# First stage: spreading the last linear steps over all half-steps of the banded attention

## The reference

```python
h = modulate(rmsnorm(x, norm1_g), shift1, scale1)
q, k, v, rw, gl = jnp.split(h @ w_in, IN_SPLITS, axis=-1)
q = apply_rope(q.reshape(B, L, N_Q_HEADS, HEAD_DIM), cos, sin)
k = apply_rope(k.reshape(B, L, N_KV_HEADS, HEAD_DIM), cos, sin)
ya = latent_window_attention(q, k, v, kc, vc, sink)
```

## Time and profile before

| what | value |
|---|---|
| median of 3 runs | 3562.92 us (3561.78 to 3563.11) |
| profiled execution, its time | 3547.06 us |
| profiled execution, its span | 3545.3 us |
| PE busy in the span | 3257.0 us (92%) |
| DVE, ACT, POOL busy | 1899.5, 1156.1, 1559.4 us |
| mean granted clock of PE | 0.948 |

### The profile page before, as it was taken

How to read it: one execution, slowest core, us unless ns; L and a number is a source line. 1 busy time by engine, 2 the same in 40 slices (tenths; PEclk the granted TensorE clock), 3 DMA queues, 4 the chain that set the end, 5 groups by cost and what they waited for, 6 DMA issues and landing times. The chain is left out here.

```text
span 3545.3 us, 46174 instructions
## 1 busy us (share of the span) xinstructions
PE 3257.0 (92%) x17972; PEld 2580.0 (73%) x17972; DVE 1899.5 (54%) x2664; ACT 1156.1 (33%) x2265; POOL 1559.4 (44%) x1195
## 2 busy tenths in 40 slices
PE   5888999999799999889999999999898999999796
PEld 2666787788598988667788878887675666777565
DVE  3278874545445455587733373337412666564736
ACT  4144441333333333431211021102223665134723
POOL 1114665456144341266666666666551001654432
PEclk8988899999899999999999999999997999999898
DMA  4335555232344342343333333334434321322112
GB/s 168 79 116 149 161 152 180 88 94 70 95 127 108 98 126 62 115 147 89 89 96 95 99 90 97 95 98 105 140 104 118 85 61 40 89 82 60 48 54 78
DMA packets 524317, 358.58 MB, mean 101 GB/s; under 512 B 92497, under 2 KB 477382, under 8 KB 524102
## 3 DMA queue, kind: packets, MB, share of 16 engines
q1 hardware_dynamic: 513446, 325.22, 31.9%
q0 software_dynamic: 4608, 16.78, 1.6%
q10 hardware_dynamic: 6048, 13.63, 1.1%
HBM read 276.85 MB, written 78.18 MB: 100 GB/s over the span
## 5 line engine op out<-in xcount | busy, mean ns | idle before, releaser
L2420 PE MATMUL psum<-place,place 128*128 128x512 f32 x2126 | 862.7, 406 | 82.5 <-POOL place L2398 35.7
L2421 PE MATMUL psum<-place,place 128*128 128x512 f32 x2126 | 842.8, 396 | 0.0
L2422 PE MATMUL psum<-place,place 128*128 128x512 f32 x2126 | 842.0, 396 | 0.0
L2396 POOL CAST place<-place 128x1024 fp32r<-128x1024 f32 (+3 forms) x302 | 303.5, 1005 | 1113.8 <-PE psum L2422 656.7
L2398 POOL TENSOR_TENSOR place<-place,place 128x1024 fp32r<-128x1024 f32 (+3 forms) x302 | 693.2, 2295 | 24.2
L2420 PEld LDWEIGHTS psum<-place,place 128*128 128x128 f32 x2126 | 408.6, 192 | 199.1 <-POOL place L2398 53.8
L2421 PEld LDWEIGHTS psum<-place,place 128*128 128x128 f32 x2126 | 408.8, 192 | 90.8 <-issue 7.5
L2422 PEld LDWEIGHTS psum<-place,place 128*128 128x128 f32 x2126 | 408.0, 192 | 87.9
L662 PE MATMUL psum<-place,place 128*128 128x512 f32 (+1 forms) x712 | 288.0, 405 | 22.3 <-issue 11.6
L663 PE MATMUL psum<-place,place 128*128 128x512 f32 (+1 forms) x712 | 272.8, 383 | 0.0
L664 PE MATMUL psum<-place,place 128*128 128x512 f32 (+1 forms) x712 | 272.4, 383 | 0.0
(11 more groups left out here) (326 smaller groups left out, 5471.8 us busy)
## 6 DMA issues: line engine op xcount, KB each, us to landing
place<-in_w_mlp_up SPq DMA_DIRECT2D x64, 512.0 KB, 4.0
place<-in_w_mlp_down SPq DMA_DIRECT2D x64, 512.0 KB, 4.0
place<-in_w_out SPq DMA_DIRECT2D x48, 512.0 KB, 4.0
chunked<-place SPq DMA_DIRECT2D x64, 320.0 KB, 3.6
place<-in_w_in SPq DMA_DIRECT2D x34, 512.0 KB, 5.7
solve<-in_w_ada POOLq DMA_DIRECT2D x32, 512.0 KB, 6.2
place<-in_lru_w_in SPq DMA_DIRECT2D x32, 512.0 KB, 4.0
place<-in_mla_w_in SPq DMA_DIRECT2D x30, 512.0 KB, 4.2
```

The costliest lines, as they stand in the source:

```text
L2396: nc.gpsimd.tensor_copy(hi, raw).then_inc(self.w_split, 1)
L2420: pe.matmul(ps, self.w_hi[:, j, k, :], hi, start=(k == 0), stop=False)
L2421: pe.matmul(ps, self.w_hi[:, j, k, :], lo, start=False, stop=False)
L2422: mm = pe.matmul(ps, self.w_lo[:, j, k, :], hi, start=False, stop=(k == kt - 1))
```

## The change

The LIN slots that are left after the lead (58) are spread evenly over all 69 WIN half-steps behind it, so that the last steps lie beside the last half-steps and some half-steps in between have none. The SOLVE slots follow every third half-step in place of every third LIN slot, stand ahead of the half-step's LIN slot, and are all given out inside the loop. No program is changed, only the list.

```diff
     order.append(LIN)
-    taken, w = first_single + 1, 0
+    taken = first_single + 1
     beside = [1, 2, 2, 2, 2, 2, 2, 2]
-    while w < win.slots or taken < lin.slots:
-        if w < win.slots:
-            order.append(WIN)
-        for _ in range(beside[w] if w < len(beside) else 1 if w < win.slots else lin.slots - taken):
-            if taken < lin.slots:
-                order.append(LIN)
-                taken += 1
-                if w >= len(beside) and taken % 3 == 0:
-                    solve(given)
-        w += 1
+    first_share = first_single + 1 + sum(beside)
+    shared, over = lin.slots - first_share, win.slots - len(beside)
+    for w in range(win.slots):
+        order.append(WIN)
+        if w < len(beside):
+            until = taken + beside[w]
+        else:
+            until = first_share + shared * (w + 1 - len(beside)) // over
+            if w % 3 == 0:
+                solve(given)
+        order += [LIN] * (until - taken)
+        taken = until
+    assert taken == lin.slots
     while solved < solver.slots:
         solve(given)
```

## The result

The changed kernel takes 3571.95 us in the median of 20 runs, the kernel before 3557.45 us in the median of 20, that is 14.5 us (0.4%) more. The ratio of the runs is 1.0037, with a 95% interval of 1.0021 to 1.0052; one run of the changed kernel, which took 16006.38 us for a reason that nothing here shows, is left out of it. The forecast was 9.2 us slower and 3572 us. That the time itself was met to 0.1 us is luck: the median of before fell by 5.5 us when 3 runs became 20, and the loss was 5.3 us larger than forecast. The loss is the better test.

What follows compares the result with a forecast made beforehand. TensorE bounds the stage while linear steps last, then a chain of waits. A tail gain of 14.3 us less 15.5 for waits, 4 for scalings and 4 for clock gave 9.2 us slower, 3572 us; range 3556 to 3583.

Steps and rivals of the forecast that it cites:

- (c): Shifted pairs: a first half waits for the PSUM bank behind ScalarE's eviction; nine places, 5.9 us lost.
- (d): Hole (half-step without a linear step) 45, behind a first half: values wait for ScalarE's last copy, 0.4 us.
- (e): Holes 33, 39, 51: eviction delays ScalarE's exponentials and the copy behind them, so values wait; 2.2 us each, 6.6 lost.
- (b): Even holes 20, 26, 58, 64: turn_last waits for ScalarE's first copy; 0.4 us each, 1.6 lost.
- (a): Half-step 8: unit 0 has one linear step where it had two, too short for its chain; 1.0 us lost.
- (f): Turns of units behind holes wait for VectorE's scalings, stretched beside GpSimd; 4 us taken, ends 0 and 11.
- (g): Idle gaps at holes 33, 39, 51 drop TensorE's clock to 1.2 GHz; two falls of 2.0, 4 us, ends 0 and 10.
- The tail is simply filled: Rival: engines off TensorE have more slack, so most of the tail's 14.3 us stays; 11 us faster, 3552; chance 0.12.
- Gain and waits cancel: Rival: holes cost (a) to (e), while (f) and (g) are hidden or the clock holds; 3562 to 3564 us; chance 0.38.
- the clock falls at more places: Rival: the clock also falls at the holes of (b) and (d), four more falls at 2.5; 3582 us; chance 0.10.
- what costs nothing: GpSimd's order of weight splits and solver chunks at the memory tiles stays; SP's waits are covered; no cost.
- Holes: Experiments' rival: a half-step without a linear step costs the same wherever it lies; only their number counts.

Runs made afterwards that it cites:

- c0: The kernel before, unchanged, run once more for a second profile: stretch (window's first mask to next stage's first load) 307.35 us, against 310.19 in the first.
- e5: Before's order with one half-step without a linear step, at 8, all later steps one half-step later, solver by count as before: ratio 1.0054 to before, stretch 334.12 us.
- e1: The changed kernel with the holes at odd half-steps 33, 39, 45, 51 moved to 34, 40, 46, 52: ratio 1.0037 to before, stretch 320.78 us.
- e8: e1 with all remaining solver chunks put behind the window: one run, window 291.65 us, 8.5 less than in e1.
- e2: The changed kernel with the hole at half-step 8 moved to 12: ratio 1.0010 to before, stretch 315.86 us.
- e4: The kernel before with its linear steps kept and only the change's new solver order: ratio 1.0012 to before, stretch 313.86 us.
- e9: Changed order with ten holes in pairs, four around the memory-keys tiles, no solver chunk at half-steps 22 to 37: ratio 0.9971 to before, stretch 294.46 us.
- e11: e9 with, in SP's list alone, the window's half-step behind the linear step that follows it: ratio 0.9955 to before, 3543.14 us, stretch 292.57 us.
- e3: The changed kernel with ten holes in pairs at even half-steps of neighbouring units, solver as in the change: ratio 0.9998 to before, stretch 304.78 us.
- e6: e3 with no solver chunk at half-steps 25 to 35, where the memory tiles lie: ratio 0.9972 to before, stretch 304.00 us.
- e7: The kernel before with its linear steps kept and no solver chunk at half-steps 22 to 32: ratio 0.9982 to before, stretch 303.39 us.
- e10: e9 with the memory tiles one unit later, behind SP's ya store, and holes moved to match: ratio 1.0006 to before, stretch 307.13 us.

## Why the prediction was right, and where its sizes were off

The sum can be held against the waits, term by term.

| term | predicted, us | shown by after, us |
|---|---|---|
| gain at the tail | 14.3 | 15.1 |
| (c) first halves behind evictions, nine | 5.9 | 5.5 |
| (d), (e) values for ScalarE's last copy | 7.0 | 7.9 |
| (b) turn_last | 1.6 | 1.0 |
| (a), (f) turn for VectorE's scaling | 5.0 | 3.6, and 0.8 beside it |
| (g) clock | 4 | 8.5 |
| splits of the memory weights | 0 | 2.6 |

The gain shown is 8.4 us of waits of before other than the memory's (14.4 in all, less 5.2 and 0.8), 3.3 at the end (from TensorE's last matmul to the next stage's first load pass 7.5 us before and 4.2 after, where the prediction had 4.7; its parts make 4.6) and 3.4 for the half of the earlier trace rows's 6.8 us at 0.50 in the tail. The clock's 8.5 are half of the four new pieces, 17.0 us, and a little too much, since TensorE was idle for 1.2 of them. Against these stand 1.7 for a shorter piece at the memory keys (6.8 us after, 10.2 before) and 0.4 for one wait fewer behind a memory eviction. The rows give 5.5 + 7.9 + 1.0 + 4.4 + 8.5 + 2.6 - 15.1 - 1.7 - 0.4 = 12.7 of the 15.7 us by which the stretch grew. The other 3.0 lie nearly all in TensorE's busy time, which grew by 6.1 where the clock pieces give 8.5 - 1.7 - 3.4 = 3.4; the profile doesn't say why, and c0 shows that the stretch itself scatters by as much.

*Right.* The tail is filled, and what it gives is eaten by waits in an in-order queue. (c), (d), (e) and the end of the stage came in the places and nearly in the sizes forecast; e5 shows (c) in 25 places, and e1 and the ScalarE rows show (e). "The tail is simply filled" fell with them: ScalarE does not start the exponentials ahead of the eviction. "Gain and waits cancel" fell because (f) and (g) were not hidden.

*Mis-sized: (f) and (g).* The prediction spread (f) over twelve places and named holes 20, 26 and 58 as its sign. No turn waited for VectorE there: of the 3.6 us in two waits 3.13 lie at hole 8 and the rest behind hole 14. What hole 8 costs as a chain that is too short was priced rightly at 1.0 us: in e5 and e8, which keep it, the first unit takes 4.69 us where before has 6.66, so that of the 2.83 us of the step left out 0.86 are lost again, 0.27 of them at the turn. TensorE's row in e8:

```profile
652.07 1.09 PE L1321 MATMUL psum<-mats,place 128*128 128x128 f32 x8 [0.27 <-DVE place L1462]
```

In after and e1 the weight split (its cast, L618) began 0.05 and 0.14 us ahead of the first scaling there, and the scalings took 3.74 and 3.65 us; in e8 and e5 it began 0.57 and 0.88 us behind it, and they took 0.88. Why the split comes earlier in the one pair than in the other is open. That (a) and (f) still add up to nearly 5.0 is luck.

(g) had two falls at 2.0 us; there were four, behind idle gaps of 3.13, 2.21, 2.45 and 2.39 us, 1.7 to 3.4 each. This is inside its own ends, 0 and 10, and not the rival "the clock falls at more places", since none came at the places that this one named. Gaps of the same size did not lose the clock elsewhere, at a keys tile of after and behind hole 51 in e2:

```profile
745.27 0.39 PE L662 MATMUL psum<-place,place 128*128 128x256 f32 x1 [2.49 <-POOL place L620]
```

```profile
861.83 1.31 PE L1295 MATMUL psum<-place,place 128*64 128x128 f32 x20 [2.38 <-ACT place L1384]
```

So neither the two falls forecast nor the four that came are fixed by the order alone.

*Held in sum, not in its parts: "what costs nothing".* GpSimd's order of splits and solver chunks at the memory tiles did stay. One chunk stands between the splits of the third and the fourth tile in both kernels (before, then after):

```profile
708.09 5.86 POOL L1134 TENSOR_TENSOR solve<-solve 128x256 f32<-128x256 f32 x8
```

```profile
751.47 4.52 POOL L1134 TENSOR_TENSOR solve<-solve 128x192 f32<-128x192 f32 x8
```

Yet TensorE's wait for the fourth tile's split rose from 2.15 to 4.40 us. GpSimd took as long from the end of the second tile's split to the end of the fourth's (14.40 us before, 14.18 after), but TensorE came to the fourth tile sooner, 9.77 us after its wait for the second in place of 12.26: in before the clock had fallen at that wait, in after it had not (c0, with the fall, has 12.30, and e1 and e2, without it, 10.09 and 9.78). So the 2.6 us more of waits for splits stand mostly against the clock's 1.7, and what TensorE loses at the memory tiles grew by some 0.5 us only. e4 shows how dear a chunk becomes (13.6 us in one unit) when it stands ahead of the values tiles. SP's queue was said to be covered too; that held in after, but e9 to e11 show a ya store in front of the memory weights as soon as the units there are short.

"Holes", the rival of the experiments, fell: with the same work, ten to eleven holes give stretches from 292.57 to 325.85 us by their places and by the order of the solver and of SP; e3, with the solver as in after, has a ratio of 0.9998 whose interval does not meet that of after. How much of a ratio belongs to which place is less sure, since e1's ratio equals after's in spite of a stretch 5.1 us shorter, and e6's gain doesn't show in its profile.

The rule that the prediction took from the Trainium skill, "SBUF — State Buffer", section "Who interferes with whom", agrees with the rows of e1 and e8: VectorE's operations there end 0.02 us behind GpSimd's subtraction. It reaches further than the scalings for which the prediction had used it, since a small operation ahead of ScalarE's exponentials, held for 1.8 to 2.1 us, delays the whole chain.

## What to carry to other kernels

Filling a tail by spreading work thinner gains only what the places can bear from which the work is taken, so at every such place go through each engine's in-order queue (what stands behind the eviction, the split, the store) before counting the gain. Put the gaps where TensorE waits anyway, keep steps that belong together in pairs, and keep other work of GpSimd away from the splits that TensorE waits for: here the three together turned 0.4% slower (after) into 0.3% faster (e9). What each gives is less sure: pairs and the solver's place have 0.9972 without the memory keys (e6), the solver's place alone 0.9982 (e7), with intervals that overlap e9's. Then read the DMA queue like an engine's, since a store that stands in front of a load shows only when all else is in time (e11, 0.9955 after 0.9971, with overlapping intervals).

## What the runs showed of the hardware

Whether an idle gap costs TensorE its clock is not told by its length alone. In the stretches of these kernels 31 gaps of 1.35 us or more were followed by 1.2 GHz, during the gap or up to 1.6 us behind it, and 14 were not: one of 1.35 us was (e6), one of 2.69 us was not (e2), and all eleven of 2.92 us or more were. What a fall costs depends on where it comes. At most places it lasts 3.4 or 6.8 us. Ahead of the memory values (128-column matmuls, each with its own weight load) it lasted 13.6, 23.9 and 27.3 us in e3, e4 and e10, with TensorE busy for 13.10, 23.72 and 26.66 us of them: being busy did not bring the clock back there. There a wait of 1.35 to 3.43 us made a unit 7 to 16 us longer (22.38 to 30.82 us in e6, e3, e4 and e10, where before has 15.04).
